# The last layer norm of a streaming encoder step: y written through accumulating DMAs onto rows of b

## The reference, cut to what matters

```python
def layer_norm(x, g, b):
    mu = jnp.mean(xf, axis=-1, keepdims=True)
    var = jnp.mean(jnp.square(xf - mu), axis=-1, keepdims=True)
    y = (xf - mu) * lax.rsqrt(var + LN_EPS) * g + b
...
h = layer_norm(ALPHA * h + moe_ffn(h, ...), ln2_g[l], ln2_b[l])   # per layer
y_prompt = h[:, N_META:]       # (1, 256, 1024)
y_sample = hs                  # (8, 16, 1024)
```

## Time and profile before

| | us |
|---|---|
| median of 3 runs | 985.69 (984.58 to 986.54) |
| the profiled execution's own time | 984.61 |
| its span in the profile | 982.8 |
| busy in it: PE / DVE / ACT / POOL | 942.2 / 822.3 / 657.1 / 259.2 |

### The profile page before, as it was taken

One profiled execution on the slowest core, in us unless ns is written; L12 is line 12 of the kernel. 1 busy time (PEld: TensorE's weight loads), 2 busy tenths in 40 slices (PEclk: granted clock), 3 DMA queues, 4 the chain that ended last, 5 costly groups with the idle time before them and its releaser, 6 DMA issues. The chain is left out here.

```text
span 982.8 us, 15259 instructions
## 1 busy us (share of the span) xinstructions
PE 942.2 (96%) x5118; PEld 782.8 (80%) x5118; DVE 822.3 (84%) x1211; ACT 657.1 (67%) x941; POOL 259.2 (26%) x343
## 2 busy tenths in 40 slices
PE   4999999999999999999989999999999999999994
PEld 3898868688888888888878988788888888888883
DVE  7878667789989989899984676588999898998996
ACT  4346541278888888888754566317888888888882
POOL 1423443471111111110223333435311111111012
PEclk9999999999999999999999999999999999999997
DMA  9863851499999999999895033529999999999865
GB/s 352 280 172 111 255 194 58 162 367 407 381 371 370 362 368 366 366 373 340 220 287 178 30 132 129 198 76 354 409 403 375 368 369 368 371 359 378 322 202 145
DMA packets 85550, 278.28 MB, mean 283 GB/s; under 512 B 8771, under 2 KB 11067, under 8 KB 85470
## 3 DMA queue, kind: packets, MB, share of 16 engines
q1 hardware_dynamic: 66880, 240.40, 66.6%
q0 software_dynamic: 11040, 21.14, 7.5%
q10 hardware_dynamic: 7566, 15.96, 4.7%
HBM read 266.51 MB, written 30.37 MB: 302 GB/s over the span
## 5 line engine op out<-in xcount | busy, mean ns | idle before, releaser
L1558 DVE TENSOR_TENSOR w_lo<-ring,w_hi 128x1024 fp32r<-128x1024 f32 x256 | 303.1, 1234 | 35.9 <-ACT w_hi L2192 33.5
L2192 ACT ACTIVATE w_hi<-ring 128x1024 fp32r<-128x1024 f32 x256 | 261.6, 1060 | 39.5 <-PE PS L1087 26.6
L1039 PE MATMUL PS<-w_hi,x_hi 128*128 128x512 f32 x512 | 163.9, 401 | 0.0
L1044 PE MATMUL PS<-w_lo,x_hi 128*128 128x512 f32 x512 | 160.4, 394 | 0.0
L1039 PE MATMUL PS<-w_hi,x_lo 128*128 128x512 f32 x512 | 160.4, 394 | 0.0
L1565 DVE TENSOR_TENSOR w_lo<-ring,w_hi 128x1024 fp32r<-128x1024 f32 x128 | 153.6, 1220 | 4.4 <-ACT w_hi L2205 4.4
L2205 ACT ACTIVATE w_hi<-ring 128x1024 fp32r<-128x1024 f32 x128 | 135.6, 1061 | 29.6 <-PE PS L1044 27.9
L2545 POOL DMA_INDIRECT M<-xs,idx x30 | 57.2, 1907 | 233.5 <-PE PS L1018 202.2
L1039 PEld LDWEIGHTS PS<-w_hi,x_lo 128*128 128x128 f32 x512 | 96.4, 188 | 23.2
L1044 PEld LDWEIGHTS PS<-w_lo,x_hi 128*128 128x128 f32 x512 | 96.5, 189 | 22.2
L1039 PEld LDWEIGHTS PS<-w_hi,x_hi 128*128 128x128 f32 x512 | 93.9, 189 | 19.5
(11 more groups left out here) (292 smaller groups left out, 1602.9 us busy)
## 6 DMA issues: line engine op xcount, KB each, us to landing
ring<-in_w_gate SPq DMA_DIRECT2D x32, 2048.0 KB, 14.1
ring<-in_w_down SPq DMA_DIRECT2D x32, 2048.0 KB, 14.8
ring<-in_w_up SPq DMA_DIRECT2D x32, 2048.0 KB
ring<-in_w_in SPq DMA_DIRECT2D x8, 2048.0 KB, 17.7
ring<-in_w_out SPq DMA_DIRECT2D x4, 2048.0 KB, 8.9
ys<-H SPq DMA_DIRECT2D x2, 3072.0 KB, 20.1
H<-ys POOLq DMA_DIRECT2D x12, 512.0 KB, 7.9
M<-in_cache_k ACTq DMA_DIRECT2D x8, 512.0 KB, 5.4
```

The source lines that it names most:

```text
L1039: pe.matmul(PS[:, n, :], x[:, c:c + P], w_hi[j][:, k * 512:(k + 1) * 512], start=(j == 0 and k == 0 and x is x_hi[par]), stop=False)
L1044: mm = pe.matmul(PS[:, n, :], x_hi[par][:, c:c + P], lo[:, k * 512:(k + 1) * 512], start=False, stop=(j == 3 and k == 1))
L1558: dve.tensor_tensor(lo, w, w_hi[j][:, :].bitcast(F32), ALU.subtract).then_inc(up_lo, 1)
L2192: act.activation(w_hi[j][:, :], quarter(3 * par + n, j)[0], ACT.Copy).then_inc(up_hi, 1)
```

## The change

- In layer 0, behind the second fill of ys with zeros, SP issues three more DMAs: the row b of the last norm (in DRAM) is written 128 times over each of the three tiles of y (in DRAM). The semaphore `y_base` counts them.
- In the end, DVE no longer runs `shifted`. It runs `mean_taken` of tiles 0 and 1, `gained` of tile 0, `mean_taken` of tile 2, `gained` of 1 and 2. Each `gained` has a buffer of its own (two in N, one in QK), so none waits for a buffer.
- ACT runs a new `end_scaled` for each tile: it multiplies the buffer, in place, by column 15 (a Copy activation with a per-row scale). Its order is `squared_rows` 0 and 1, `end_scaled` 0, `squared_rows` 2, `end_scaled` 1 and 2.
- POOL runs `row_power` 0 and 1, then an accumulating DMA of buffer 0 to y, `row_power` 2, the accumulating DMA of buffer 1 and that of buffer 2. Each DMA waits for its `end_scaled`. They add the buffer to what stands in DRAM, which is b.
- SP's three stores of H to y are gone; SP still waits for the three DMAs that write y.

```diff
@@ SP, layer 0, behind the zeros of ys @@
+                        if half == 1:
+                            for j in range(3):
+                                sp.dma_start(y_rows(j), t["ln2_b"][DEPTH - 1].partition_broadcast(P)).then_inc(y_base, 16)
@@ SP, the end @@
-            for j in tiles_of(DEPTH - 1):
-                dst = o["y_prompt"][0, P * j:P * (j + 1), :] if j < 2 else o["y_sample"].rearrange("b t n -> (b t) n")
-                sp.wait_ge(h_done, ln_count(LN2[-1], j))
-                sp.dma_start(dst, H[:, j, :]).then_inc(y_out, 16)
             sp.wait_ge(y_out, 48)
@@ DVE @@
-                return did(dve.scalar_tensor_tensor(gained_rows[n % 2][p], H[p, j, :], stats[p, j, 13:14],
-                                                    gb_two[p, 0, :], ALU.add, ALU.mult))
-            def shifted(l, n, c):
...
+                dve.scalar_tensor_tensor(end_rows[n], H[p, j, :], stats[p, j, 13:14], gb_two[p, 0, :], ALU.add, ALU.mult
+                                         ).then_inc(end_gained, 1)
...
-                    for n in range(len(tiles_of(l))):
-                        mean_taken(l, n)
-                    gain_at = gained(l, 0)
-                    for n in range(len(tiles_of(l))):
-                        shifted(l, n, gain_at)
-                        if n + 1 < len(tiles_of(l)):
-                            gain_at = gained(l, n + 1)
+                    mean_taken(l, 0)
+                    mean_taken(l, 1)
+                    gained(l, 0)
+                    mean_taken(l, 2)
+                    gained(l, 1)
+                    gained(l, 2)
@@ ACT @@
+            def end_scaled(l, n):
+
+                act.wait_ge(end_gained, n + 1)
+                act.wait_ge(ln_rstd, ln_count(LN2[l], n))
+                act.activation(end_rows[n], end_rows[n], ACT.Copy, scale=stats[:, order(LN2[l])[n], 15:16]
+                               ).then_inc(y_scaled, 1)
...
+                    squared_rows(l, 0)
+                    squared_rows(l, 1)
+                    end_scaled(l, 0)
+                    squared_rows(l, 2)
+                    end_scaled(l, 1)
+                    end_scaled(l, 2)
@@ POOL @@
+                row_power(l, 0)
+                row_power(l, 1)
+                pool.wait_ge(y_base, 48)
+                for n in range(3):
+                    if n == 1:
+                        row_power(l, 2)
+                    pool.wait_ge(y_scaled, n + 1)
+                    pool.dma_start(y_rows(order(LN2[l])[n]), end_rows[n], accum_op=ALU.add).then_inc(y_out, 16)
```

More of the change, by code:

```diff
@@ L295, in program @@
         gained1 = Z1
-        gained_rows = [N[:, 2816 + 1024 * i:3840 + 1024 * i] for i in range(2)]
         xs = nc.dram_tensor("xs", (NTOK, D), F32, kind="Internal").ap()
@@ L346, in program, with y_rows @@
         comb = sem("combined")
-        y_out = sem("y_out")
+        y_out, y_base, end_gained, y_scaled = sem("y_out"), sem("y_base"), sem("end_gained"), sem("y_scaled")
+        def y_rows(j):
+            return o["y_prompt"][0, P * j:P * (j + 1), :] if j < 2 else o["y_sample"].rearrange("b t n -> (b t) n")
+        end_rows = [N[:, 2816:3840], N[:, 3840:4864], QK[:, 0:1024]]
         rank_moved = sem("rank_moved")
@@ L2302, in moe_round @@
                     result(PAIRS - 1, 1, 0)
+            def end_scaled(l, n):
[3 more added lines that the diff above has]
+                               ).then_inc(y_scaled, 1)
             def closing(l, rb):
                 if l + 1 == DEPTH:
-                    for n in range(len(tiles_of(l))):
-                        squared_rows(l, n)
+                    squared_rows(l, 0)
[4 more added lines that the diff above has]
+                    end_scaled(l, 2)
                     return
@@ L2473, in row_power, with row_powers @@
                 pool.tensor_tensor(st[:, 15:16], st[:, 14:15], half[0:TN[j], 0:1], ALU.pow).then_inc(ln_rstd, 1)
+            def row_powers(l):
+                if l + 1 < DEPTH:
+                    for n in range(4):
+                        row_power(l, n)
+                    return
+                row_power(l, 0)
[6 more added lines that the diff above has]
+                    pool.dma_start(y_rows(order(LN2[l])[n]), end_rows[n], accum_op=ALU.add).then_inc(y_out, 16)
             def results_added(l):
@@ L2662, in _ @@
                 with pool.If(more < 1):
-                    for n in range(len(tiles_of(l))):
-                        row_power(l, n)
+                    row_powers(l)
                 steps[0] = done
```

## The result

The change makes the kernel slower: 990.89 us (989.61 to 992.05, 4 runs) against 985.32 (984.58 to 986.54, 4 runs), a ratio of 1.0059 with a 95% interval of 1.0041 to 1.0077. Forecast were 986.9 and a range up to 990.2; the first median lies above that range, the second just inside it.

What follows compares the result with a forecast made beforehand. TensorE was taken as the bound for most of the span, DVE's chain and the store at the end. Issue 3.0 us earlier, then 6.8 us instead of 2.6 to landing, gave +1.2 us: 986.9 us, range 984.3 to 990.2.

Steps and rivals of the forecast that it cites:

- the span ends 0.7 us behind the landing: End of the kernel: a 0.7 us tail after y's last landing, counted the same before and after the change.
- the early issue of the last DMA: At the end: last DMA of y issued at 976.5 instead of 979.5, 3.0 us earlier, from the shorter DVE chain.
- The accumulating DMAs: POOL's DMAs into y: 5.4 us to landing for one alone, 2.6 us more behind another; 6.8 us for the last.
- Rival (b): Last accumulating DMA is cheap, landing in 3.0 to 5.4 us: 0.2 to 2.6 us faster; chance 0.17.
- Rival (a): Accumulating DMA into DRAM has a long tail, 9.4 us to landing: 986.6 span, 3.8 us slower; chance 0.32.
- DVE, ACT and POOL at the end: DVE done at 974.5, third sum 0.16 us later, ACT's copies 1.1 us each, last DMA issued at 976.5.
- POOL held by DVE: Tile 2's reciprocal: POOL's first instruction held by `gained` 2 until 974.53, second takes 0.55 us, reciprocal ready at 975.2.
- rival (c): POOL not held by `gained` 2, last DMA out at 975.7: span 983.2, 0.4 us slower; chance 0.05.
- The early part: Layer 0's three early DMAs: costed at nothing, cache_k having 8.5 us of room; at most 7.4 us without cover.
- Rival (d): Early writes delay the loads of layer 0: up to 7.4 us slower; chance 0.04.

Runs made afterwards that it cites:

- e6: Kernel before with DVE's end reordered, last `shifted` and store halved, and tile 2's reciprocal moved from POOL to ACT and DVE: 983.38 us, ratio 0.9976.
- e11: Kernel before in its own order with whole stores; only tile 2's reciprocal moved from POOL to ACT and DVE: ratio 1.0002.
- e4: Changed kernel without early writes, SP storing the scaled rows by plain DMAs, POOL left its small instructions (y lacks b): 984.13 us, ratio 0.9983 against before.
- e3: Changed kernel without early writes, POOL's three DMAs storing instead of accumulating (y lacks b): 986.19 us, ratio 1.0009 against before.
- e8: Changed kernel with its third accumulating DMA cut to 64 of 1024 columns: ratio 1.0027 against before.
- e1: Kernel before plus only the three early DMAs writing b to y, and SP's wait for them before its stores: ratio 0.9995.
- e9: The changed kernel repeated unaltered against the kernel before: 990.01 us against 985.69, ratio 1.0041 (1.0029 to 1.0053).
- e7: Kernel before with DVE's end reordered, a third buffer, last `shifted` and store halved; POOL keeps tile 2's reciprocal: 984.90 us, ratio 0.9990.
- e5: Kernel before plus a one-element memset as POOL's last instruction, waiting for the last `shifted`: 989.22 us, ratio 1.0043.

## Why the prediction was wrong

- **The step that failed** is the term "the span ends 0.7 us behind the landing", used for before and carried over to after. It was no fixed tail. In before the last of the 0.7 us was the remainder of POOL's drain, begun at 975.0 (in e6 and e11, where that drain was over early, the span ended 0.4 to 0.5 us behind the landing); in after the tail was 3.6 us, since the DMA that lands last is now POOL's own. That is 2.9 of the 4.1 us; the other 1.2 us are the forecast. By the same error the prediction took the early issue of the last DMA as a gain of 3.0 us on the way to the end. e4 shows what that is worth with the plain store kept: the end is 1.1 us shorter (11.4 us from the third sum instead of 12.5), not 3.0, and POOL's drain holds the rest.
- **The accumulating DMAs** were sized rightly in their sum, from rows 7: 5.4 us each for the first two, 6.8 for the third where I had 6.8. That this last figure fits so well is luck: I had 5.4 and 2.6 us, less the 1.2 us between the two issues; measured were 5.4 and 3.0, less 1.6. The fit of the Trainium skill, "DMA: Bandwidth & Descriptors", section "Anatomy of one DMA — SWDGE (gpsimd) path", gives an estimate of 3.2 us for 512 KB; the trace agrees for the plain store from POOL (3.4 us in e3) and not for the addition (5.4 us). Rival (b) is out by the 6.8 us.
- **Rival (a)** came close to the measured time (989.5 on the scale of the medians), but not by its mechanism: it wanted a landing of 9.4 us. That the result lies near it is a coincidence of sums.
- **DVE, ACT and POOL at the end** went nearly as worked out: last issue 6.2 us behind the third sum where I had 6.0 (976.5 less 970.47), ACT's copies 1.15 us against 1.1. The third sum was not delayed by `gained` 0 in after: that ended at 972.57, before the landing at 972.64. In e3, e4, e6 and e8, where the landing came sooner behind the second sum, it was bound by it.
- **POOL held by DVE** went as forecast, though no run isolates the cause: the first small instruction of tile 2 took 1.07 us beside `gained` 2, the second, begun 0.13 us after that had ended, 0.55. So rival (c) did not happen.
- **The early part** was costed at nothing, with the 8.5 us of room behind cache_k as the reason. In e1 that was right. In after it was not: the prediction looked at cache_k, which landed after 13.4 us instead of 8.1 and still in time, but not at cache_v, issued behind it, for which TensorE waited 1.4 us (0.3 in e9). Rival (d) happened in small. The 2.4 us by which the third sum came later in the profiled execution of after is within what executions differ by (e4, without early writes, had it at 972.6; e9 at 971.8), and the upper bound of the repeat, 5.2 us, leaves room for no more than about 1 us beside the 4.1 us of the end. How much of the wait for cache_v reaches the end is open, and so is why e1, with the same early writes, does not show it.

## What to carry to other kernels

Before shortening the chain that ends last, look at the closing instructions of every engine, which neither the chain of waits nor the busy groups show: here GpSimd's drain, 6.6 us behind its last instruction, ended 0.5 us after the landing that seemed to set the end. So GpSimd's last work, however small, and above all its last DMA belong well ahead of the last store, and the last bytes should leave by a hardware queue; move a small late instruction to an engine whose drain takes 0.1 us. That alone gave nothing here (e11), since DVE's chain ended almost as late; with a shorter chain it gave 2.3 us (e6), where the shorter chain alone gave 1 us by the runs and 0.2 by the trace (e7). An addition that a DMA makes costs 5.4 us to landing for 512 KB, and 6.8 behind another, where the plain store of the same tile took 2.6 to 3.4, so it must not be the last thing. And where early DMAs are hidden in a busy stretch, follow every load that is in flight there to its first reader, not one of them.

## What the runs showed of the hardware

- POOL's closing DRAIN lasted until 6.5 to 6.8 us behind its last instruction in nine of the twelve profiled executions, also where that instruction was a memset of one element (e5, 6.6 us) and where its last DMA had landed long before (e4, landing at 972.5, drain over at 983.8).
- Behind DMAs of its own that land late, the drain was over 3.3 to 3.4 us after the landing (985.7 to 989.1, 985.0 to 988.4, 981.9 to 985.3).
- An accumulating DMA from SBUF into DRAM took as long as one from DRAM into SBUF: 5.4 us for the first and for the second, issued 2.9 us behind it; the third, issued 1.6 us behind the second, landed 3.0 us behind it. The DMA engines were full at 185 GB/s from 977.5 to 982 in after, where one plain store had 406.
- Beside 1.5 MB written from DRAM to DRAM, loads of 512 KB on ACT's queue landed later: cache_k after 12.0 to 13.4 us instead of 7.6 to 8.4, cache_v after 14.6 to 16.3 us instead of 8.4 to 9.1.
